# The last layer normalisation of a mixer-and-MoE layer on ScalarE and VectorE alone, without GpSimd

## The reference

```python
def layer_norm(x, g, b):
    xf = x.astype(F32)
    mu = jnp.mean(xf, axis=-1, keepdims=True)
    var = jnp.mean(jnp.square(xf - mu), axis=-1, keepdims=True)
    return ((xf - mu) * lax.rsqrt(var + LN_EPS) * g + b).astype(x.dtype)
...
    h = layer_norm(DEEPNORM_ALPHA * h + ffn, ln2_g[l], ln2_b[l])
```

## Time and profile before

| | us |
|---|---|
| median of 3 runs | 2163.17 |
| lowest and highest run | 2161.89, 2163.58 |
| span of the profiled execution, first to last instruction | 2158.9 |
| busy in the span: PE | 2069.2 (96%) |
| busy: DVE | 1086.9 (50%) |
| busy: ACT | 423.6 (20%) |
| busy: POOL | 703.4 (33%) |

### The profile page before, as it was taken

How to read it: one execution, slowest core, us unless ns; L and a number is a source line. 1 busy time by engine, 2 the same in 40 slices (tenths; PEclk the granted TensorE clock), 3 DMA queues, 4 the chain that set the end, 5 groups by cost and what they waited for, 6 DMA issues and landing times. The chain is left out here.

```text
span 2158.9 us, 23073 instructions
## 1 busy us (share of the span) xinstructions
PE 2069.2 (96%) x7129; PEld 1093.2 (51%) x7130; DVE 1086.9 (50%) x2963; ACT 423.6 (20%) x909; POOL 703.4 (33%) x612
## 2 busy tenths in 40 slices
PE   7999999999999999999999999899999999999990
PEld 6445887574644555554444554444444444444440
DVE  6121445549451222212224656776666666666647
ACT  2111333334321111112221221011111111111112
POOL 1752002212032221203351001455445545545533
PEclk9999999999999999999999999999999999999995
DMA  5421000012122121126335004799999999999964
GB/s 147 115 87 39 20 20 20 20 45 73 45 74 78 54 69 56 61 71 226 98 103 205 30 40 165 282 340 355 347 348 355 361 357 358 350 354 354 349 197 157
DMA packets 129902, 368.24 MB, mean 171 GB/s; under 512 B 34333, under 2 KB 66193, under 8 KB 104353
## 3 DMA queue, kind: packets, MB, share of 16 engines
q1 hardware_dynamic: 104224, 312.64, 38.8%
q0 software_dynamic: 23520, 54.61, 10.5%
q10 hardware_dynamic: 2080, 0.01, 0.1%
HBM read 318.37 MB, written 68.16 MB: 179 GB/s over the span
## 5 line engine op out<-in xcount | busy, mean ns | idle before, releaser
L2993 PE MATMUL banks<-arena 128*128 128x512 f32 x1056 | 471.2, 599 | 5.8 <-DVE arena L2986 3.5
L2972 POOL DMA_INDIRECT arena<-h_rows,index x268 | 276.7, 1033 | 155.6 <-issue 76.8
L2993 PEld LDWEIGHTS banks<-arena 128*128 128x128 f32 x1056 | 196.2, 191 | 230.2 <-issue 226.2
L1712 PE MATMUL banks<-arena 128*128 128x512 f32 x616 | 279.7, 596 | 0.4 <-ACT arena L329 0.4
L3009 PE MATMUL banks<-arena 128*128 128x512 f32 x528 | 237.6, 592 | 1.3 <-ACT arena L2808 0.8
L285 PE MATMUL banks<-arena 128*128 128x512 f32 x480 | 221.9, 600 | 3.3 <-PEq L108 3.0
L2986 DVE STREAM_TRANSPOSE arena<-arena 128x1024 f32<-128x1024 f32 x66 | 133.9, 2028 | 135.2 <-PE banks L2993 135.2
L2980 POOL DMA_INDIRECT sums<-arena,row_to x66 | 107.1, 1623 | 271.1 <-DMA sums<-arena,row_to 247.1
L1712 PEld LDWEIGHTS banks<-arena 128*128 128x128 f32 x616 | 110.5, 190 | 116.1 <-issue 115.1
L3009 PEld LDWEIGHTS banks<-arena 128*128 128x128 f32 x528 | 100.2, 190 | 127.0 <-issue 125.3
L2956 DVE TENSOR_SCALAR index<-row 32x1 uint32<-32x1 f32 x1072 | 155.4, 145 | 17.1
(11 more groups left out here) (392 smaller groups left out, 2384.6 us busy)
## 6 DMA issues: line engine op xcount, KB each, us to landing
arena<-in_w_exp_gate_dram SPq DMA_DIRECT2D x66, 1024.0 KB
arena<-in_w_exp_up_dram SPq DMA_DIRECT2D x66, 1024.0 KB
arena<-in_w_exp_down_dram SPq DMA_DIRECT2D x66, 1024.0 KB
arena<-in_w_in_dram SPq DMA_DIRECT2D x26, 1024.0 KB, 5.2
gates<-arena SPq DMA_DIRECT2D x60, 256.0 KB, 2.0
arena<-gates SPq DMA_DIRECT2D x60, 256.0 KB, 2.6
arena<-h_rows,index POOLq DMA_INDIRECT x268
arena<-in_x_dram SPq DMA_DIRECT2D x8, 512.0 KB, 6.0
```

Of the source, the lines that this page charges most:

```text
L1712: mm = pe.matmul(gate_bank(n, b), left[:, k, :], right[:, k, :], start=(alone and k == 0), stop=(k == 3), skip_group_check=True)
L2972: return pool.indirect_dma_start(w.x[k][:, 256 * q:256 * (q + 1)], None, rows, bass.IndirectOffsetOnAxis(ap=g.index[:, k, q:q + 1], axis=0 ...
L2993: mm = pe.matmul(g.bank[:, 2, :].rearrange("p (a f) -> p a f", a=2), xT[:, k, :], wgu[:, :, k, :], start=(k == 0), stop=(k == KT - 1))
```

## The change

Only the body of `finish` changes, and GpSimd has no part left in it. Tile 0 keeps `bn_stats` and `bn_aggr` on VectorE. For tiles 1 to 7 ScalarE makes the sums: one pass `Copy` over the tile with an accumulated output gives the sum of its values, and after VectorE has made the negative mean of it, one pass `Square` with that mean as its bias and an accumulated output gives the sum of the centred squares. What these passes write (`scratch`) is not used. VectorE then does both products, (z - mean) * g2 and xn * rstd + b2, in the order: mean of tile m, second product of tile m-1, first product of tile m, variance of tile m. The line numbers of the changed file: L3058 is the mean (`middle`), L3062 the variance (`spread`), L3069 the first product (`gain`), L3074 the reciprocal and L3079 the second product (`bias`), L3095 the square root (`deviation`), L3099 the pass that sums and L3102 the pass that squares.

```diff
--- before.py
+++ after.py
@@ -3024,9 +3024,11 @@
     xn = [g.region(at + D * i, D) for i in range(2)]
     res = [g.region(at + 2 * D + D * i, D) for i in range(3)]
     at += 5 * D
-    stats = g.region(at, NT, 2, 6)
-    mv, rstd = g.region(at + 128, NT, 2), g.region(at + 160, NT)
-    s = {n: sem("f_" + n) for n in "st ag ve g2 sd rs xn b2 end".split()}
+    stats = g.region(at, 2, 6)
+    mv = g.region(at + 32, 2)
+    total, square, mean, rstd = (g.region(at + 64 + 16 * i, NT) for i in range(4))
+    scratch = [g.region(RING[1] + D * i, D) for i in range(2)]
+    s = {n: sem("f_" + n) for n in "st ag to sq me ve sd rs xn b2".split()}
     sum_in = [sem(f"sum_in{m}") for m in range(NT)]
     out_done = [sem(f"out_done{i}") for i in range(3)]
 
@@ -3035,49 +3037,74 @@
         for m in range(NT):
             sp.dma_start(z[:, m, :], g.sums[m * P:(m + 1) * P, :]).then_inc(sum_in[m], 16)
         for m in range(NT):
-            if m < NT - 1:
-                sp.wait_ge(s["b2"], m + 1)
-            else:
-                sp.wait_ge(s["end"], 1)
+            sp.wait_ge(s["b2"], m + 1)
             sp.dma_start(g.out[0, m * P:(m + 1) * P, :], res[m % 3]).then_inc(out_done[m % 3], 16)
         for k in range(3):
             sp.wait_ge(out_done[k], 16 * len(range(k, NT, 3)))
 
     def vector(dve):
-        dve.wait_ge(g.gb_in, 32)
-        for m in range(NT):
-            dve.wait_ge(sum_in[m], 16)
+        def first_tile():
+            dve.wait_ge(sum_in[0], 16)
             for h in range(2):
-                dve.bn_stats(stats[:, m, h, :], z[:, m, h * HALF:(h + 1) * HALF]).then_inc(s["st"], 1)
-            dve.wait_ge(s["st"], 2 * m + 2)
-            dve.bn_aggr(mv[:, m, :], stats[:, m]).then_inc(s["ag"], 1)
-            dve.wait_ge(s["ag"], m + 1)
-            dve.tensor_scalar(rstd[:, m:m + 1], mv[:, m, 1:2], LN_EPS, None, ALU.add).then_inc(s["ve"], 1)
+                dve.bn_stats(stats[:, h, :], z[:, 0, h * HALF:(h + 1) * HALF]).then_inc(s["st"], 1)
+            dve.wait_ge(s["st"], 2)
+            dve.bn_aggr(mv, stats).then_inc(s["ag"], 1)
+            dve.wait_ge(s["ag"], 1)
+            dve.tensor_scalar(mean[:, 0:1], mv[:, 0:1], -1.0, None, ALU.mult).then_inc(s["me"], 1)
+            dve.tensor_scalar(rstd[:, 0:1], mv[:, 1:2], LN_EPS, None, ALU.add).then_inc(s["ve"], 1)
+
+        def middle(m):
+            dve.wait_ge(s["to"], m)
+            dve.tensor_scalar(mean[:, m:m + 1], total[:, m:m + 1], -1.0 / D, None, ALU.mult).then_inc(s["me"], 1)
+
+        def spread(m):
+            dve.wait_ge(s["sq"], m)
+            dve.tensor_scalar(rstd[:, m:m + 1], square[:, m:m + 1], 1.0 / D, LN_EPS,
+                              ALU.mult, ALU.add).then_inc(s["ve"], 1)
+
+        def gain(m):
+            dve.wait_ge(s["me"], m + 1)
             if m >= 2:
                 dve.wait_ge(s["b2"], m - 1)
-            dve.scalar_tensor_tensor(out=xn[m % 2], in0=z[:, m, :], scalar=mv[:, m, 0:1], in1=g2,
-                                     op0=ALU.subtract, op1=ALU.mult).then_inc(s["g2"], 1)
+            dve.scalar_tensor_tensor(out=xn[m % 2], in0=z[:, m, :], scalar=mean[:, m:m + 1], in1=g2,
+                                     op0=ALU.add, op1=ALU.mult).then_inc(s["xn"], 1)
+
+        def bias(m):
             dve.wait_ge(s["sd"], m + 1)
             dve.reciprocal(rstd[:, m:m + 1], rstd[:, m:m + 1]).then_inc(s["rs"], 1)
-        m = NT - 1
-        dve.wait_ge(s["xn"], NT)
-        dve.wait_ge(out_done[m % 3], 16 * (m // 3))
-        dve.tensor_tensor(res[m % 3], xn[m % 2], b2, ALU.add).then_inc(s["end"], 1)
+            dve.wait_ge(s["rs"], m + 1)
+            dve.wait_ge(s["xn"], m + 1)
+            if m >= 3:
+                dve.wait_ge(out_done[m % 3], 16 * (m // 3))
+            dve.scalar_tensor_tensor(out=res[m % 3], in0=xn[m % 2], scalar=rstd[:, m:m + 1], in1=b2,
+                                     op0=ALU.mult, op1=ALU.add).then_inc(s["b2"], 1)
+
+        dve.wait_ge(g.gb_in, 32)
+        first_tile()
+        gain(0)
+        for m in range(1, NT):
+            middle(m)
+            bias(m - 1)
+            gain(m)
+            spread(m)
+        bias(NT - 1)
 
     def scalar(act):
-        for m in range(NT):
+        def deviation(m):
             act.wait_ge(s["ve"], m + 1)
             act.activation(rstd[:, m:m + 1], rstd[:, m:m + 1], ACT.Sqrt).then_inc(s["sd"], 1)
-            act.wait_ge(s["g2"], m + 1)
-            act.wait_ge(s["rs"], m + 1)
-            act.activation(xn[m % 2], xn[m % 2], ACT.Copy, scale=rstd[:, m:m + 1]).then_inc(s["xn"], 1)
+
+        for m in range(1, NT):
+            act.wait_ge(sum_in[m], 16)
+            act.activation(scratch[0], z[:, m, :], ACT.Copy, accum_out=total[:, m:m + 1]).then_inc(s["to"], 1)
+            deviation(m - 1)
+            act.wait_ge(s["me"], m + 1)
+            act.activation(scratch[1], z[:, m, :], ACT.Square, bias=mean[:, m:m + 1],
+                           accum_out=square[:, m:m + 1]).then_inc(s["sq"], 1)
+        deviation(NT - 1)
 
     def gpsimd(pool):
-        for m in range(NT - 1):
-            pool.wait_ge(s["xn"], m + 1)
-            if m >= 3:
-                pool.wait_ge(out_done[m % 3], 16 * (m // 3))
-            pool.tensor_tensor(res[m % 3], xn[m % 2], b2, ALU.add).then_inc(s["b2"], 1)
+        pass
 
     part = Shared()
     part.sync, part.vector, part.scalar, part.gpsimd = sync, vector, scalar, gpsimd
```

## The result

| us | before | after |
|---|---|---|
| median of 4 runs each | 2163.21 | 2149.72 |
| lowest, highest | 2161.89, 2163.58 | 2147.65, 2153.44 |
| span of the profiled execution | 2158.9 | 2145.9 |

The ratio is 0.9941 (95% interval 0.9929 to 0.9954): 0.59% faster, 13.5 us between the medians. The forecast was 2150.6, between 2148.6 and 2153.6.

What follows compares the result with a forecast made beforehand. VectorE was taken to bound the last stage, standing for GpSimd's additions. First to last product 10.1 us less, the end 2.7 less, first product 0.12 later: 2163.17 - 12.6 = 2150.6 us, range 2148.6 to 2153.6.

Steps and rivals of the forecast that it cites:

- VectorE is the bound and 1.94 us of a tile is a hidden wait for GpSimd: Last stage before the change: VectorE's product stands, booked as busy, until GpSimd's addition ends, about 1.94 us in seven tiles.
- 3.01 us a tile: VectorE's steady loop after the change, from one tile's variance to the next: 3.01 us, where a tile took 4.82 before.
- Tile 0 and the table load: Stage start: ScalarE's table load, formerly in idle time, now delays tile 0's deviation, costing VectorE about 1.0 us once.
- a second load: Rival at ScalarE's table switch: it costs twice its row, a second 1.28 us added once, total 2151.9 us; chance 0.05.
- the further drain of about 1.38 us: Skill's cost for each ScalarE table switch besides the load, 2.66 us in all; it would make the sum 1.4 us longer.
- ScalarE has 0.2 to 0.4 us to spare: Steady tile: ScalarE's square root and two passes take about 2.6 us with reads overlapped, leaving 0.2 to 0.4 us spare.
- No new wait for the stores: Stage's stores: one every 3.0 us, landing in 2.6 us, 4.4 at most while loads run, so VectorE never waits.
- The 9 us which the prediction gave the buffers: Result buffers of the last stage: said to come round after 9 us, so no new wait for a store.
- The sum: VectorE's last instruction ends at 2143.16 instead of 2155.79 us, 12.6 us less, giving 2150.6 us or -0.58%.
- The 4.27 us above the span: Median before lies 4.27 us above the profiled execution's 2158.9 us span; this difference was carried over unchanged.

Runs made afterwards that it cites:

- b1: Kernel before, with the bias of tiles 0 to 6 added by VectorE instead of GpSimd: stage 32.47 us against 39.25, ratio to before 0.9958.
- b2: Kernel before, with GpSimd adding the bias only to the first 512 of 1024 values of tiles 0 to 6: stage 31.72 us against 39.25.
- a1: Changed kernel, with an unused GpSimd addition of 128x1024 put back beside each of tiles 0 to 6: stage 37.88 us, ratio to before 0.9995.
- a0: The changed kernel run again unaltered: median 2149.86 us, from 2148.24 to 2153.04, stage 26.47 us against 26.63.
- a2: Changed kernel, with a square root of a constant column ahead of ScalarE's first summing pass, so the table load comes early: stage 26.32 us, median 2146.22.
- a7: a2's kernel with two result buffers instead of three: stage 28.63 us, median 2154.47 us.
- a4: Changed kernel, with the first product of tile m ahead of the reciprocal and second product of tile m-1: stage 24.94 us, ratio to before 0.9937.
- a5: Changed kernel with early table load, first product ahead, and last tile's second product and store in halves: stage 24.80 us, ratio to before 0.9928.
- a6: a5's kernel with four result buffers: stage 24.80 us, median 2148.61 us.

## Why the prediction was right

- **VectorE is the bound and 1.94 us of a tile is a hidden wait for GpSimd.** Right, and shown by b1, b2 and a1: the product falls to 1.28 us when GpSimd is empty, by 1.08 us when the addition is 1.08 us shorter, and rises again to 2.98 us when the additions come back beside other code.
- **3.01 us a tile.** Measured 3.01 (2125.84 to 2128.85), with each step of the loop within 0.02 us: square root 0.18 after the variance, reciprocal 0.23 after that, product 0.20, product 1.20, variance 1.20. The small steps came from tile 0 and from the norm of the routing stage, which has the same instructions in another order.
- **Tile 0 and the table load.** Expected 1.0 us of wait; 0.96 us measured, 0.80 in a0, and a2 took it off. That nothing as large as a second load comes with it was right (1.40 us of ScalarE's time for a row of 1.28); the further drain of about 1.38 us which the Trainium skill ("ScalarE: Activation LUTs", What ACT_TABLE_LOAD costs) counts is not in this trace, where the read of the accumulator, the load and the square root follow each other within 0.02 us.
- **ScalarE has 0.2 to 0.4 us to spare.** Too low: it waits 0.64 us a tile. The prediction took each part too long by a little. `Square` starts 0.11 us after the square root does and not after its full 0.20, and a pass with its read takes 1.13 us, not 1.15 + 0.1 or 1.06 + 0.1: the read starts 1.04 us into `Square` and 0.94 us into `Copy`, and the next pass 0.09 us after the read (`Square` at 2126.13, `Copy` at 2127.26). Together ScalarE works 2.37 us a tile where 2.6 were taken. It changed nothing here.
- **No new wait for the stores.** Right for the changed kernel, but nearer than thought. The term that was mis-sized is the landing of a store beside the loads: I took 4.4 us at most from before, and it was 6.0 us after and 8.3 us in a2. With three buffers a store has 7.7 us (three tiles of 3.01 us less the 1.3 us of the product before its issue); a2 missed that by 0.78 us, the waits for the landing included. The 9 us which the prediction gave the buffers was the time from product to product and not from issue to need.
- **The sum.** 12.6 us expected, 12.62 us in the stage time. So close an agreement is luck in part, since the stage of the same kernel was 26.63 us once and 26.47 the other time; but its terms agree too: from the first product to the second tile's 3.72 us (3.71 expected), and from the last first product to the end 3.09 (3.09). The medians differ by 13.5 us; the rest is within the spread of what comes ahead of the stage (a0).
- **The 4.27 us above the span.** This step I put wrongly. The changed kernel's profiled execution took 2147.65 us with a span of 2145.9, so 1.75 us lie around the span, and so it is in each of these profiles that has its own time (a1: 2161.25 and 2159.5). If it was so before too, the other 2.5 us are a profiled execution below its median. As the saving was taken off the median, it didn't matter.

## What to carry to other kernels

An instruction that is much longer than the same instruction elsewhere in the trace may be a wait booked as busy time: compare durations by form, and look at which other engine's instruction ends a fixed time before it does. Where VectorE is the bound, an elementwise addition given to GpSimd to help it can cost more than doing it on VectorE, here 1.94 us of standing against 1.2 us of work. And when a stage is shortened, ask of each transfer in it how late it may land: the first store here landed 4.4 us after its issue before, and 8.3 us after it once its result was ready 2.2 us earlier in the stage and the loads were still running.

## What the runs showed that I had not expected

- GpSimd's fill of 128x1024 (0.94 us with 0.16 us of overlap, 0.95 with 0.62) runs beside VectorE's two-input product at no cost that can be seen to either, while its addition stops it for as long as it lasts (1.26 us for 512 values a partition, 2.35 us for 1024), and the product then takes 1.08 us to its end whichever the length.
- The first store, issued while the eight loads of 512 KB still ran, landed in 4.4 us before, in 6.0 and 6.4 us in the changed kernel, in 7.6 and 8.3 us where only the table load is early too (a7, a2), and in 4.6 to 6.2 us in a4, a5 and a6. Once the loads are done a store lands in 2.6 us; the second one still took 4.9 us in the changed kernel and 6.3 in a2.
- Runs of one kernel differed by up to 7.7 us (a2: 2145.35 to 2153.00). The profile of the slowest of them has 5.6 us of its time over the changed kernel's ahead of the stage, where the code is the same.
